# Decoder layer on one core: gated norm and the first output unit's halves moved to other attention steps

## What is computed

```
qp, kp, vp, up = project_mixer(rms_norm(y_p, g_mix_pre), w_in)
att = finish_diff_heads(diff_attention(q, k, v, lam), g_subln)      # 4 heads, 2 softmaxes each, ALiBi
y   = gelu(s5_mix(u))
y   = y * sigmoid(y @ w_glu)
y   = rms_norm(y, g_ssm_out)                                        # the "gated norm"
y_p = y_p + rms_norm(concat([att, y]) @ w_out, g_mix_post)
```

## Time and profile before

| | us |
|---|---|
| median of 3 runs | 991.49 |
| lowest and highest | 990.19, 991.56 |
| the profiled execution's own time | 988.71 |
| its span, first to last instruction | 986.5 |
| mean granted TensorE clock in it | 0.985 |

### The profile page before, as it was taken

One profiled execution on the slowest core, in us unless ns is written; L12 is line 12 of the kernel. 1 busy time (PEld: TensorE's weight loads), 2 busy tenths in 40 slices (PEclk: granted clock), 3 DMA queues, 4 the chain that ended last, 5 costly groups with the idle time before them and its releaser, 6 DMA issues.

```text
span 986.5 us, 18130 instructions
## 1 busy us (share of the span) xinstructions
PE 942.6 (96%) x7734; PEld 876.2 (89%) x7734; DVE 443.1 (45%) x900; ACT 356.3 (36%) x565; POOL 170.9 (17%) x46
## 2 busy tenths in 40 slices
PE   3999999899899999999899999999999999999997
PEld 2999998776699999976379999999999999999996
DVE  5799975765354677111453572222222222001103
ACT  5442224574454463135334543222222222222111
POOL 3000000000000001300030003433333333353330
PEclk9999999889999999999899989999999999999999
DMA  7304205342251358358051101222222232222202
GB/s 213 109 34 130 87 2 199 123 130 87 86 171 54 124 171 295 132 213 341 1 171 44 43 28 60 85 85 85 87 91 94 96 100 75 86 76 75 86 33 91
DMA packets 85343, 105.85 MB, mean 107 GB/s; under 512 B 9473, under 2 KB 72834, under 8 KB 85154
## 3 DMA queue, kind: packets, MB, share of 16 engines
q1 hardware_dynamic: 85056, 104.92, 32.0%
...
## 4 chain that ended last, share of the span: by engine, by line
PE 86%; DVE 8%; ACT 3%; issue 2%; DMA 1%; ACTq 0%; DVEq 0%
PE pall L1796 55%; PE pall L1808 7%; PE pall L2130 5%; PE pall L1833 4%; PE pall L2177 2%; PE pall L1820 2%; PE pall L2188 1%; PE pall L1886 1%; PE pall L1986 1%; DVE a_s L1434 1%; PE pall L1869 1%; PE pall L1890 1%; PE pall L2224 1%; PE pall L1995 1%; PE pall L1852 1%
## 5 line engine op out<-in xcount | busy, mean ns | idle before, releaser
L627 POOL TENSOR_TENSOR w_lo<-w_raw,w_hi 128x2048 fp32r<-128x2048 f32 (+1 forms) x36 | 161.2, 4476 | 622.8 <-ACT w_hi L670 332.1
L1796 PE MATMUL pall<-x_hi,w_hi 128*128 128x272 f32 x1024 | 213.5, 290 | 0.0
L1796 PE MATMUL pall<-x_lo,w_hi 128*128 128x272 f32 x1024 | 212.0, 288 | 0.0
L1796 PE MATMUL pall<-x_hi,w_lo 128*128 128x272 f32 x1024 | 210.6, 287 | 0.0
L1796 PEld LDWEIGHTS pall<-x_lo,w_hi 128*128 128x128 f32 x1024 | 161.5, 189 | 0.0
L1796 PEld LDWEIGHTS pall<-x_hi,w_hi 128*128 128x128 f32 x1024 | 160.5, 189 | 0.8
L1796 PEld LDWEIGHTS pall<-x_hi,w_lo 128*128 128x128 f32 x1024 | 160.6, 189 | 0.0
L670 ACT ACTIVATE w_hi<-w_raw 128x2048 fp32r<-128x2048 f32 (+1 forms) x61 | 114.7, 1880 | 91.4 <-PE pall L1796 91.4
L1796 PE MATMUL pall<-g_hi,w_hi 128*128 128x272 f32 x352 | 73.1, 289 | 0.0
L1796 PE MATMUL pall<-g_lo,w_hi 128*128 128x272 f32 x352 | 72.7, 288 | 0.0
L1796 PE MATMUL pall<-g_hi,w_lo 128*128 128x272 f32 x352 | 72.6, 287 | 0.0
...
## 6 DMA issues: line engine op xcount, KB each, us to landing
...
```

Of the source, the lines that this page charges most:

```text
L627: e.tensor_tensor(w_lo[:, n % 2, 0:w], w_raw[:, n % 2, 0:w], w_hi[:, n % 2, 0:w].bitcast(F32), ALU.subtract)\
L1796: ins = mm(acc(j)[:, a, :], w, x[:, k_x + k, a * HALF:(a + 1) * HALF], start=first and k == 0 and s_, stop=last and k == kts - 1 and t_)
```

## The change

The list is laid out anew, and three small things follow from it.

- `glu` 3 goes from ahead of the steps into step 2, behind the scores of block 2.
- `first_out` leaves its place ahead of `glu` 2. ACT's half is now in step 12; DVE's half gets a name of its own, `first_lo`, in step 14. `out_hi` goes from step 12 to 15.
- `ssm_root` goes from step 3 to step 4, its sums to bank 3; two `keep_busy` calls (4 and 6) and three waits around it are gone.
- `ssm_rows` goes from step 4 to 9, `ssm_t` 0 to 3 from steps 4, 4, 5, 6 to 10, 11, 11, 12, `ssm_l` from 7 to 13. `ssm_t` reads the rows out of PSUM, so ACT's copy to `rstd` is gone.
- `hsum` 0 and 1 go from steps 9 and 11 to 13, since they use bank 7, which the rows hold until the fourth tile is scaled.

```diff
-    order += [..., ("att", 0), ("exp", 0), ("glu", 0), ("glu", 1), ("att", 1), ("exp", 1), ("atd", 0),
-              ("first_out", 0), ("glu", 2), ("glu", 3)]
-    between = {2: [("dkt", 0), ("dkt", 1)], 3: [("dkt", 2), ("dkt", 3), ("dqz", 0), ("ssm_root", 0)], 4: [("ssm_rows", 0), ("ssm_t", 0), ("dkt", 4), ("dkt", 5), ("ssm_t", 1), ("dkt", 6), ("dkt", 7)],
-               5: [("ssm_t", 2), ("dks", 0), ("dkt", 8), ("dkt", 9)], 6: [("ssm_t", 3), ("dsm", 0), ("dkt", 10), ("dkt", 11)],
-               7: [("ssm_l", 0), ("dsc", 0), ("dpt", 0), ("dkt", 12), ("dkt", 13)], 8: [("dpe", 0), ("dv", 0), ("dkt", 14), ("dkt", 15)],
-               9: [("do", 0), ("dot", 0), ("dks", 1), ("hsum", 0)], 10: [("dsm", 1)], 11: [("dsc", 1), ("dpt", 1), ("hsum", 1)], 12: [("dpe", 1), ("dv", 1), ("out_hi", 0)],
-               13: [("do", 1)], 14: [("dot", 1)], 15: [("hsum", 2)],
-               16: [("out_s5", 0)]}
+    order += [..., ("att", 0), ("exp", 0), ("glu", 0), ("glu", 1), ("att", 1), ("exp", 1), ("atd", 0), ("glu", 2)]
+    between = {2: [("glu", 3), ("dkt", 0), ("dkt", 1)], 3: [("dkt", 2), ("dkt", 3), ("dqz", 0)],
+               4: [("dkt", 4), ("dkt", 5), ("ssm_root", 0), ("dkt", 6), ("dkt", 7)], 5: [("dks", 0), ("dkt", 8), ("dkt", 9)],
+               6: [("dsm", 0), ("dkt", 10), ("dkt", 11)], 7: [("dsc", 0), ("dpt", 0), ("dkt", 12), ("dkt", 13)],
+               8: [("dpe", 0), ("dv", 0), ("dkt", 14), ("dkt", 15)], 9: [("do", 0), ("dot", 0), ("dks", 1), ("ssm_rows", 0)],
+               10: [("dsm", 1), ("ssm_t", 0)], 11: [("dsc", 1), ("dpt", 1), ("ssm_t", 1), ("ssm_t", 2)],
+               12: [("dpe", 1), ("dv", 1), ("ssm_t", 3), ("first_out", 0)], 13: [("do", 1), ("ssm_l", 0), ("hsum", 0), ("hsum", 1)],
+               14: [("dot", 1), ("first_lo", 0)], 15: [("hsum", 2), ("out_hi", 0)], 16: [("out_s5", 0)]}
...
-            elif kind == "ssm_rows":
-                e.wait_ge(S("norm_rows"), 1)
-                e.activation(two(rstd[:]), halves(6), ACT.Copy).then_inc(S("rstd_half"), 1)
...
-                e.wait_ge(S("rstd_half"), 1)
-                mul(uT[:, n, :], uT[:, n, :], rstd[:]).then_inc(S("norm_t"), 1)
+                e.wait_ge(S("norm_rows"), 1)
+                mul(two(uT[:, n, :]), two(uT[:, n, :]), halves(6)).then_inc(S("norm_t"), 1)
...
+            if h == 0:
+                e.wait_ge(S("norm_t"), SF)
...
                 elif n == 4:
-                    keep_busy(bank(3), 6)
-                    e.wait_ge(S("rstd_half"), 1)
-                elif n >= 6 or 2 <= n < 4:
+                    e.wait_ge(S("dkT_done"), 4)
+                elif n >= 2:
                     e.wait_ge(S("dkT_done"), n - 1)
...
-                keep_busy(bank(3), 4)
                 e.wait_ge(*counted("ssmn", "add", SF - 1))
-                e.wait_ge(S("dkT_done"), 4)
                 for c in range(8):
-                    ins = mm(bank(6)[0:CHUNK, 300 + c:301 + c], ...)
+                    ins = mm(bank(3)[0:CHUNK, 320 + c:321 + c], ...)
```

More of the change, by code:

```diff
@@ L380, in build @@
     order += [("y1", f) for f in range(SF - 1)]
-    order += [("s5y", 3), ("y1", SF - 1), ("s5_end", 0), ("att", 0), ("exp", 0), ("glu", 0), ("glu", 1), ("att", 1), ("exp", 1), ("atd", 0),
-              ("first_out", 0), ("glu", 2), ("glu", 3)]
-    between = {2: [("dkt", 0), ("dkt", 1)], 3: [("dkt", 2), ("dkt", 3), ("dqz", 0), ("ssm_root", 0)], 4: [("ssm_rows", 0), ("ssm_t", 0), ("dkt", 4), ("dkt", 5), ("ssm_t", 1), ("dkt", 6), ("dkt", 7)],
-               5: [("ssm_t", 2), ("dks", 0), ("dkt", 8), ("dkt", 9)], 6: [("ssm_t", 3), ("dsm", 0), ("dkt", 10), ("dkt", 11)],
-               7: [("ssm_l", 0), ("dsc", 0), ("dpt", 0), ("dkt", 12), ("dkt", 13)], 8: [("dpe", 0), ("dv", 0), ("dkt", 14), ("dkt", 15)],
-               9: [("do", 0), ("dot", 0), ("dks", 1), ("hsum", 0)], 10: [("dsm", 1)], 11: [("dsc", 1), ("dpt", 1), ("hsum", 1)], 12: [("dpe", 1), ("dv", 1), ("out_hi", 0)],
-               13: [("do", 1)], 14: [("dot", 1)], 15: [("hsum", 2)],
-               16: [("out_s5", 0)]}
+    order += [("s5y", 3), ("y1", SF - 1), ("s5_end", 0), ("att", 0), ("exp", 0), ("glu", 0), ("glu", 1), ("att", 1), ("exp", 1), ("atd", 0), ("glu", 2)]
+    between = {2: [("glu", 3), ("dkt", 0), ("dkt", 1)], 3: [("dkt", 2), ("dkt", 3), ("dqz", 0)],
[5 more added lines that the diff above has]
+               14: [("dot", 1), ("first_lo", 0)], 15: [("hsum", 2), ("out_hi", 0)], 16: [("out_s5", 0)]}
     for n in range(2, len(ATT) + 2):
@@ L889, in _ @@
                 e.wait_ge(*counted("ssmn", "sum", 1))
-                e.activation(small[0:CHUNK, 8:16], bank(6)[0:CHUNK, 300:308], ACT.Sqrt, bias=small[0:CHUNK, EPS_COL:EPS_COL + 1])\
+                e.activation(small[0:CHUNK, 8:16], bank(3)[0:CHUNK, 320:328], ACT.Sqrt, bias=small[0:CHUNK, EPS_COL:EPS_COL + 1])\
                     .then_inc(S("norm_root"), 1)
-            elif kind == "ssm_rows":
-                e.wait_ge(S("norm_rows"), 1)
-                e.activation(two(rstd[:]), halves(6), ACT.Copy).then_inc(S("rstd_half"), 1)
             elif kind == "ssm_t":
@@ L1459, in _ @@
                         ins.then_inc(S("dqz"), 1)
-            elif kind == "first_out":
+            elif kind == "first_lo":
                 split_lo()
@@ L1717, in pair_half @@
             mul((sq if up else tt)[:, m, in_half(a)], bank(i)[:, 0:HALF], rstd[:, in_half(a)]).then_inc(acc_out, 1)
-        e.wait_ge(S("rstd_half"), 1 + 1)
+        e.wait_ge(S("rstd_half"), 1)
         for i in range(4):
@@ L1725, in _ @@
         recip_half("n4", 1)
-        e.wait_ge(S("rstd_half"), 1 + 2)
+        e.wait_ge(S("rstd_half"), 2)
         for i in range(4, 8):
@@ L2018, in _ @@
                     e.wait_ge(S("dqz"), 8)
-                    e.wait_ge(S("k_tok_ready"), 5)
+                    e.wait_ge(*counted("ssmn", "root", 1))
                 else:
@@ L2087, in _ @@
                 e.wait_ge(S("k_tok_ready"), 5)
-                keep_busy(bank(3), 4)
                 e.wait_ge(*counted("ssmn", "add", SF - 1))
-                e.wait_ge(S("dkT_done"), 4)
                 for c in range(8):
-                    ins = mm(bank(6)[0:CHUNK, 300 + c:301 + c], sqacc[:, c * CHUNK:(c + 1) * CHUNK], ones[:, 0:1], start=True, stop=True)
+                    ins = mm(bank(3)[0:CHUNK, 320 + c:321 + c], sqacc[:, c * CHUNK:(c + 1) * CHUNK], ones[:, 0:1], start=True, stop=True)
                 ins.then_inc(S("norm_sum"), 1)
@@ L2095, in _ @@
                 e.wait_ge(S("norm_recip"), 1)
+                e.wait_ge(S("dkT_done"), 16)
                 for c in range(8):
@@ L2293, in _ @@
             elif i >= 6:
-                e.wait_ge(S("rstd_half"), 1 + i - 5)
+                e.wait_ge(S("rstd_half"), i - 5)
             half_product(bank(i), (wx_hi[s_], wx_lo[:, s_, :]), i % 2, a, during_first(i))
```

## The result

The changed kernel takes **997.64 us** (median of 4 runs, 996.74 to 999.64) where the kernel before takes 990.84 beside it: a ratio of 1.008, 95% interval 1.0065 to 1.0095. That is 6.8 us slower. The forecast was 995.9, slower by 4.4. The profiled execution took 997.09 us, its span is 994.9 (before 986.5), so the two profiles differ by 8.4 us, and it is these that are taken apart here. PE is TensorE, DVE is VectorE and ACT is ScalarE, as in the texts of the runs. A "stretch", or a low stretch, is time in which the granted clock is 1.2 GHz, and a "fall" is its start.

What follows compares the result with a forecast made beforehand. PE, 96% busy, bounds the whole, but in the attention steps waits between PE and DVE and the granted clock count. Terms sum to -1.4, plus 5.8 for the clock: +4.4, so 995.9 us against the median; range 989.5 to 1000.5.

Steps and rivals of the forecast that it cites:

- steps 7, 9, 10 to 12, 13 and 14 to 15: Terms for moved work and waits of PE and DVE: -0.8, +0.8, +2.2, +1.2 and +2.2 us, in that order.
- The clock in steps 12 to 16: Forecast for steps 12 to 17: two new half-clock stretches of 6.9 us behind PE's gaps, 2.9 each, +5.8 us.
- Steps 2 to 5: Early attention steps: block 6 comes 8.8 us earlier at full clock, less 1.8 for half clock, net -7.0 us.
- one stretch of 6.9 us: Half clock from about 192 instead of two such stretches, its cost mostly hidden behind DVE: +1.8 us.
- The bound of -2.5: Smallest early gain, if half clock lasts through step 5, doubling its 4.87 us and the 0.65 to 1 before it.
- Rival C: Half clock lasts through steps 4 and 5, as transposes don't raise it: -2.5 for -7.0, sum +8.9, 1000.4 us; chance 0.15.
- Rival A: The two later gaps, in steps 12 and 15, bring no fall or one: -1.4 or +1.5, 990.1 or 993.0 us; chance 0.20.
- rival B: Steps 2 to 5 gain 8.8 and no fall comes in steps 12 and 15: sum -3.2, 988.3 us; chance 0.12.
- Theories A and B: From the experiments: A, clock falls follow PE's waits (no wait, no fall); B, waits cost only themselves, low stretches come anyway.

Runs made afterwards that it cites:

- r1_tiles_step9: The changed kernel with the root's rows ahead of the second decode scores, `ssm_t` 0 to 2 in step 9, tile 3 in 10, `ssm_l` in 11: 995.6 us.
- r4_tile3_step12: The changed kernel with tiles 0 to 2 in step 9, the output unit's two parts in step 8, tile 3 and `ssm_l` ending step 12: 988.56 us.
- r5_fill_late: The changed kernel with idle-time matmuls in PE's late waits, ahead of the decode values, `att_p` 13's transposes and the output product: 991.88 us, ratio 1.0020.
- r7_fill_early: The changed kernel with idle-time matmuls in four early waits of PE, 4, 2, 3 and 2 calls: 995.54 us, ratio 1.0057.
- r6_unit_step2: The changed kernel with both parts of the first output unit back ahead of `glu` 2's product in step 2: 995.73 us, ratio 1.0047.
- r8_all: r4_tile3_step12 and r7_fill_early together, `ssm_l` behind block 13's bias, and idle-time matmuls ahead of block 14 and the output product: 981.13 us.
- r11_norm_fill: r8_all with idle-time matmuls also in the norm ahead of the ffn: 979.17 us, ratio 0.9895.
- r0_change: The changed kernel run again with no edit, for a second profile: 999.03 us, ratio 1.0083 to the kernel before.

## Why the prediction was right, and where it was not

**Sign and mechanism.** Slower by 6.8, forecast 4.4, and the case that I held likeliest is the one that came. The waits came at the places and nearly at the sizes told: 3.17 for "about 3.4" ahead of `dv`, 1.83 and 1.12 for "1.9 and 1.4", steps 7, 9, 10 to 12, 13 and 14 to 15 within 0.1 us each. They follow from adding up DVE's operations from the earlier trace rows against its idle time, and r1_tiles_step9 to r4_tile3_step12 showed the two causes one by one by taking the operations away.

**The clock in steps 12 to 16**: +5.8 forecast, +5.8 in the profile, and 6.2 by r5_fill_late. The size is right by some luck. I had two stretches of 6.9, and there were three, of 3.3, 3.4 and 6.9, together 13.6 and so as long. That such a stretch "has" 6.9 us was read from four windows of one execution; here they took 3.3 to 13.7 us.

**Steps 2 to 5 is the term that was mis-sized.** Forecast -7.0, measured -4.6. r7_fill_early has the same order with the clock held up: 25.5 us from block 1 to block 6, where the working without a fall had 25.1. So the chain of DVE was right to 0.4, and the rest, 1.9, is the clock: charged with 1.8 ("most of it hidden behind DVE"), it costs 3.7. So the step that failed in size is "one stretch of 6.9 us", "most of it hidden behind DVE": the stretch was 10.3 us long and reached step 5, whose scores are PE's own. The bound of -2.5 for half clock through step 5 doesn't come out of its own terms either: -8.8 with 4.87 and 0.65 to 1 added is -3.3 to -2.9, and with the 1.8 of the steps before -1.5 to -1.1. Rival C's 1000.4 carries that error, of at most 1.4 us. I also had it that freeing DVE from the split was the point. r6_unit_step2 shows it as 1.3 of the gain; the 3.0 up to block 3 come with the split in its old place.

**Rival A (fewer stretches)** and **rival B (the early gain whole)** did not come by themselves. With the late waits filled, r5_fill_late is A's case: 2 us slower than the kernel before where A had 1.4 faster. In its profile the attention time is 1.3 longer (95.1 against 93.8), and 2.6 of the 2.7 between that and A's -1.4 is the early term's error (-4.4 in this profile for -7.0); behind the attention that profile lost nothing. B's condition, no fall at all in these steps, was met only by r8_all and r11_norm_fill, which have other moves besides.

**Rival C (half clock through steps 4 and 5)** is the one nearest to what was missed: the stretch did last into the sample scores of step 5, to 203.7. Its reason is not borne out. In r7_fill_early transposes and one-column matmuls alone run for 3.7 us at a clock of 1.00. The Trainium skill (TensorE: Matmul & The Clock Gate, Part 4: PE-mode transpose) would have them not count as busy; this trace speaks against it as far as holding the clock up goes, by 3.7 us of one profile, and if these rows are in that mode, which the trace doesn't say. Whether such work delays the rise, once the clock is low, no run here parts from the rest: in the kernel before it rose among them, in the change behind them.

**Behind the attention** 1.0 us was lost that the forecast had at nothing. It is the net of two. In the norm ahead of the ffn the low stretch was 10.3 us and not 6.9, and the way from its first sum to its second rows took 14.30 us in place of 11.95. In the cross-attention the low stretch was 3.4 us and not 6.9, and the values of the earlier trace rows took 5.14 us from start to start in place of 6.42. In r11_norm_fill's profile the norm's stretch is gone with its waits filled; why it is longer in some runs than in others stays open.

**Theories A and B.** Filling the waits took the stretches away in r5_fill_late, r7_fill_early, r8_all and r11_norm_fill, as A says. "No wait, no fall" is too strong: r0_change had a fall with no wait told ahead of it, and r4_tile3_step12 one behind 0.48 us.
